# Output projection as three rounded products, squares summed on VectorE, and the second norm in four groups

## The reference, cut to what matters

```
h = RMSNorm(x) * (1 + scale1) + shift1
z = h @ w_in                      # three head groups: GLA, mLSTM, S5
x = x + gate1 * (concat[A, B, C] @ w_out)        # w_out 2048 x 2048
h = RMSNorm(x) * (1 + scale2) + shift2
x = x + gate2 * PEER(h)           # w_q 2048 x 2048, then all 16384 experts' u and v
```

## Time and profile before

| | us |
|---|---|
| median of 3 runs | 4954.34 |
| the profiled execution's own time | 4968.97 |
| its span in the profile | 4967.2 |
| output projection, first to last product | 277.6 |
| from its last product to the first block product | 67.1 |

### The profile page before, as it was taken

One profiled execution on the slowest core, in us unless ns is written; L12 is line 12 of the kernel. 1 busy time (PEld: TensorE's weight loads), 2 busy tenths in 40 slices (PEclk: granted clock), 3 DMA queues, 4 the chain that ended last, 5 costly groups with the idle time before them and its releaser, 6 DMA issues.

```text
span 4967.2 us, 68686 instructions
## 1 busy us (share of the span) xinstructions
PE 4623.2 (93%) x29440; PEld 4147.1 (83%) x29440; DVE 2422.2 (49%) x3620; ACT 1000.8 (20%) x1128; POOL 638.5 (13%) x492
## 2 busy tenths in 40 slices
PE   6799999999899699999999999999986998899898
PEld 3577777776655599999999999999976998899897
DVE  0388223114300324676777611111134888788785
ACT  1000101111100211222234411111121222222222
POOL 1000000001000000000000000000044884333330
PEclk7899999987799799999999999999987999999999
DMA  7211211146611222333334433333345999999993
GB/s 300 86 52 52 74 53 64 51 157 259 260 62 49 93 75 84 100 109 109 100 131 161 159 110 99 106 108 108 101 144 195 357 353 332 344 347 337 331 334 144
DMA packets 209254, 805.62 MB, mean 162 GB/s; under 512 B 35496, under 2 KB 101480, under 8 KB 153112
## 3 DMA queue, kind: packets, MB, share of 16 engines
q1 hardware_dynamic: 151832, 526.99, 30.3%
q0 software_dynamic: 37056, 212.73, 11.5%
q10 hardware_dynamic: 20160, 62.92, 3.1%
HBM read 724.74 MB, written 77.84 MB: 162 GB/s over the span
## 4 chain that ended last, share of the span: by engine, by line
PE 84%; DMA 8%; DVE 4%; issue 3%; ACT 1%; SPq 0%; DVEq 0%; ACTq 0%
PE PS L2061 12%; PE PS L2063 12%; PE PS L2062 12%; PE PS L1935 11%; PE PS L2041 6%; PE PS L2139 5%; PE PS L2141 5%; PE PS L2140 5%; PE PS L1938 4%; DMA arena<-in_peer_v 4%; DMA arena<-in_w_ada 3%; PE PS L1707 2%; PE PS L2113 2%; DVE arena L1630 2%; PE PS L1691 1%
## 5 line engine op out<-in xcount | busy, mean ns | idle before, releaser
L2061 PE MATMUL PS<-h_hi,blk_hi 128*128 128x288 f32 x4608 | 1368.6, 297 | 58.0 <-DVE blk_lo L1466 53.8
L2063 PE MATMUL PS<-h_hi,blk_lo 128*128 128x288 f32 x4608 | 1359.3, 295 | 0.0
L2062 PE MATMUL PS<-h_lo,blk_hi 128*128 128x288 f32 x4608 | 1359.0, 295 | 0.0
L2061 PEld LDWEIGHTS PS<-h_hi,blk_hi 128*128 128x128 f32 x4608 | 866.7, 188 | 59.0 <-issue 50.6
L2062 PEld LDWEIGHTS PS<-h_lo,blk_hi 128*128 128x128 f32 x4608 | 866.8, 188 | 0.0
L2063 PEld LDWEIGHTS PS<-h_hi,blk_lo 128*128 128x128 f32 x4608 | 866.1, 188 | 0.0
L2139 PE MATMUL PS<-co_hi,ev_hi 128*128 128x384 f32 x2048 | 702.1, 343 | 120.4 <-DVE arena L1614 100.6
L1466 DVE TENSOR_TENSOR blk_lo<-arena,blk_hi 128x2048 fp32r<-128x2048 f32 x144 | 329.9, 2292 | 820.9 <-ACT blk_hi L917 820.4
L2141 PE MATMUL PS<-co_hi,ev_lo 128*128 128x384 f32 x2048 | 698.4, 341 | 22.5 <-issue 22.5
L2140 PE MATMUL PS<-co_lo,ev_hi 128*128 128x384 f32 x2048 | 698.7, 341 | 17.6 <-issue 17.6
L1935 PE MATMUL PS<-arena 128*128 128x288 f32 x2176 | 550.0, 413 | 2.2 <-ACT arena L748 2.2
(11 more groups left out here) (427 smaller groups left out, 4126.6 us busy)
## 6 DMA issues: line engine op xcount, KB each, us to landing
arena<-in_peer_ut SPq DMA_DIRECT2D x128, 1024.0 KB, 5.4
arena<-in_peer_v SPq DMA_DIRECT2D x256, 512.0 KB
arena<-in_w_ada SPq DMA_DIRECT2D x48, 2048.0 KB, 9.3
activation_scratch<-arena ACTq DMA_DIRECT2D x128, 288.0 KB, 5.4
arena<-in_w_f SPq DMA_DIRECT2D x17, 2048.0 KB, 7.8
gate_scratch<-arena ACTq DMA_DIRECT2D x12, 2048.0 KB, 7.1
arena<-activation_scratch SPq DMA_DIRECT2D x32, 768.0 KB
arena<-gate_scratch SPq DMA_DIRECT2D x32, 768.0 KB
```

The costliest lines, as they stand in the source:

```text
L2061: mm(split(k)[:, x], hi[:, c], h_part[0][:, c, cols], start=c == 0, stop=False)
L2062: mm(split(k)[:, x], hi[:, c], h_part[1][:, c, cols], start=False, stop=False)
L2063: ins = mm(split(k)[:, x], lo[:, c], h_part[0][:, c, cols], start=False, stop=c == KC - 1)
```

## The change

What it does:

1. `mix_high`, `mix_low`: as the 16 chunks of the mixed heads become ready, ACT rounds each to `mix_hi` and DVE takes the rest as `mix_lo`. Six are done in the input projection's stage, one behind each of heads 2 to 5 (and four more behind head 4), the last two behind head 5.
2. `out_high`, `out_low`: each w_out tile is split likewise, in four pieces of 1024 columns, `out_hi` into two new tiles, `out_lo` in place in the ring slot.
3. Three rounded matmuls per chunk in place of one plain one, in halves of 256 and 320 columns in place of 512 and 64. PE waits for `out_lo_made` and `mix_lo_made`.
4. Squares are made on ACT and added up on DVE (`add_square`) as the residual chunks come; PE does one product with ones at the end.
5. x is loaded before head 11 is done, and saved chunk by chunk. The three first w_q blocks are issued at the last product, the save of the last two chunks and the keys behind them.
6. The second norm and its split go in four groups of four chunks (`normed`, `normed_high`, `normed_low`); the first block product takes each chunk when its `h_lo` is there.

```diff
+            def mix_high(c):
+                act.wait_ge(hn_out if c < 12 else s5_mix, c + 1 if c < 12 else 3)
+                act.activation(mix_part[0][:, c], mix_raw[:, c], ACT.Copy).then_inc(mix_hi_made, 1)
+            def out_high(t):
+                act.wait_ge(ring_in[(Y_OUT + t) % 2], ring_fills(Y_OUT + t))
+                if t >= 2:
+                    act.wait_ge(prod_made, 2 * (t - 2) + 2)
+                for q in range(4):
+                    cols = slice(1024 * q, 1024 * q + 1024)
+                    act.activation(out_hi[t % 2][:, cols], ring_flat[(Y_OUT + t) % 2][:, cols], ACT.Copy).then_inc(out_hi_made, 1)
             ml_square(HEADS - 1)
+            mix_high(10)
             ml_root(HEADS - 1)
-            act.wait_ge(res_made, KC)
-            square_chunks(xres, sq2, 1)
+            out_high(0)
+            mix_high(11)
+            out_high(1)
+            for t in range(8):
+                for c in (2 * t, 2 * t + 1):
+                    act.wait_ge(res_made, c + 1)
+                    if c >= 2:
+                        act.wait_ge(sq_used, KC + c - 1)
+                    act.activation(sq2[:, c % 2], xres[:, c], ACT.Square).then_inc(sq_made, 1)
+                if t < 6:
+                    out_high(t + 2)
...
             ml_mean(HEADS - 1)
+            mix_low(10)
             head_out(11, m_rs)
+            out_low(0)
+            mix_low(11)
+            out_low(1)
+            for t in range(8):
+                for c in (2 * t, 2 * t + 1):
+                    residual(c)
+                    if c:
+                        add_square(c - 1)
+                if t < 6:
+                    out_low(t + 2)
...
-            dve.wait_ge(prod_out, 16 + 4)
             inverse_root(1, 3)
-            modulated(h2T[:, :].rearrange("p (c t) -> p c t", t=T), xres, V_NG2, 48, 64).then_inc(norm_made, 1)
-            dve.wait_ge(h_hi_made, 1)
-            tt(h_lo[:, :], h2T[:, :], h_hi[:, :].bitcast(F32), ALU.subtract).then_inc(h_lo_made, 1)
+            dve.wait_ge(x_saved, 16 * KC)
+            normed(0)
             low(0, 0)
+            for g in range(1, 4):
+                normed(g)
+                normed_low(g - 1)
+            dve.sem_inc(norm_made, 1)
+            normed_low(3)
             low(1, 1)
...
-                        for lo, w in ((0, TP), (TP, TS)):
+                        for b in range(2):
+                            out, cols = bank(2 * m + b, 0, (256, T - 256)[b]), slice(256 * b, (256, T)[b])
                             for c in MIX:
...
-                                ins = mm(flat(m)[:, lo:lo + w], ring[y % 2][:, c, P * m:P * m + P], mixT[:, c, lo:lo + w],
-                                         start=c == MIX[0], stop=c == MIX[-1])
+                                mm(out, hi[:, c, wc], mix_part[0][:, c, cols], start=c == MIX[0], stop=False)
+                                mm(out, hi[:, c, wc], mix_part[1][:, c, cols], start=False, stop=False)
+                                ins = mm(out, lo[:, c, wc], mix_part[0][:, c, cols], start=False, stop=c == MIX[-1])
-            sum_squares(sq2, 1, 3)
+            pe.wait_ge(sq_used, 2 * KC)
+            for lo, w in ((0, TP), (TP, TS)):
+                ins = mm(flat(3)[:, lo:lo + w], ones[:, :], sq_sum[:, lo:lo + w], start=True, stop=True)
...
+                        if isinstance(n, int) and n == 0 and x == 0:
+                            pe.wait_ge(h_lo_made, c + 1)
...
+            sp.wait_ge(prod_made, KC)
             for n in range(3):
                 load_block(a["w_q"][n], n, n)
+            save_x(14)
+            save_x(15)
```

More of the change, by code:

```diff
@@ L871, in _ @@
                         act.activation(rstd[:, :], rstd[:, :], ACT.Sqrt).then_inc(s5_sig, 1)
+                    if job == GLU_SUM // 2 + 1:
+                        for c in range(6):
+                            mix_high(c)
                     if job == ML_LOGS:
@@ L899, in _ @@
                     ada_tile_out(u)
+                if h >= 2:
+                    mix_high(6 + h - 2)
+                if h == 4:
+                    for c in range(12, 16):
+                        mix_high(c)
                 if h == 0:
@@ L950, in _ @@
             high(0, 0, 16)
+            for g in range(4):
+                normed_high(g)
             high(1, 1, 16)
@@ L1361, in _ @@
             ts(mq, mq, MDH ** -0.5, None, ALU.mult).then_inc(ml_pre, 1)
+            for c in range(6):
+                mix_low(c)
             dve.wait_ge(ml_cols, 1)
@@ L1443, in residual @@
+            mix_low(11)
+            out_low(1)
+            dve.wait_ge(x_in, 32)
+            def residual(chunk):
+                m = chunk % 2
+                xc, gcol = xres[:, chunk], mod[:, 32 + chunk]
+                pair = PS[:, 1024 * m:1024 * m + 1024].rearrange("p (b t) -> p b t", b=2)
+                dve.wait_ge(prod_made, chunk + 1)
+                step(tt(seqs(gate_tmp), seqs(pair[:, 1, 256:T - 256]), gcol[:, 1:NCOND].unsqueeze(2).broadcast_to([P, NSEQ, SLEN]),
                         ALU.mult))
-                stt(xc[:, 0:TP], flat(m)[:, 0:TP], gcol[:, 0:1], xc[:, 0:TP], ALU.mult, ALU.add).then_inc(prod_out, 1)
+                stt(halves(xc[:, 0:TP]), pair[:, :, 0:256], gcol[:, 0:1], halves(xc[:, 0:TP]), ALU.mult, ALU.add
+                    ).then_inc(prod_out, 1)
@@ L1459, in _, with add_square @@
[L1459 to L1460 removed]
+            def add_square(c):
+                dve.wait_ge(sq_made, KC + c + 1)
+                if c == 0:
+                    dve.tensor_copy(sq_sum, sq2[:, 0]).then_inc(sq_used, 1)
+                else:
+                    dve.wait_ge(sq_used, KC + c)
+                    tt(sq_sum, sq_sum, sq2[:, c % 2], ALU.add).then_inc(sq_used, 1)
+            for t in range(8):
+                for c in (2 * t, 2 * t + 1):
+                    residual(c)
+                    if c:
+                        add_square(c - 1)
+                if t < 6:
+                    out_low(t + 2)
@@ L1463, in low, with normed_low @@
+            def normed_low(g):
+                for c in range(4 * g, 4 * g + 4):
+                    dve.wait_ge(h_hi_made, c + 1)
+                    ins = tt(h_part[1][:, c], h2c[:, c], h_part[0][:, c].bitcast(F32), ALU.subtract)
+                    ins.then_inc(h_lo_made, 1)
             def low(n, k):
```

120 lines of the change are left out of this document (77 added, 43 removed).

## The result

The kernel before took 4955.92 us (median of 4 runs, 4951.11 to 4961.4) and the changed one 4892.10 us (median of 4, 4887.07 to 4896.05): ratio 0.9875, with 95% between 0.9862 and 0.9889. That is 63.8 us less, 28 us short of the 91.3 forecast and 2 us outside the forecast's range. The profiled execution of the changed kernel took 4890.59 us, 78.4 less than that of the kernel before.

A forecast was written before the change was run, and what follows sets the result against it. PE was taken as the bound (84% of the chain of waits). Products -77.6, start +12.5, clock +2.0 and tail -28.2 sum to -91.3 us, so the median 4954.34 becomes 4863 us, range 4843 to 4890.

The forecast's parts named there:

- the last one of the sum: Behind the tail: loads, stores and waits counted from block ends, so everything shifts, with no further gain or loss.
- The products: Output projection: 768 pairs of rounded products at 0.452 ns a column take 200.0 us in place of 277.6, -77.6.
- The bound from above: Projection: weight loads hold 256-column products at 130 ns, adding 11 us, 4874 in all; rival's chance 0.12.
- the rival in which the excess is absent: Projection: products cost their columns alone at 2.4 GHz, 184.3 us, 16 less, total 4847; chance 0.06.
- The start by its cause: Projection's start: PE's first product waits for all of `out_low(0)` behind head 11, at 1361.9 for 1349.4, +12.5 us.
- The clock behind the start: Projection's first products: after 12 us of rest PE runs at clock 0.50 for a while, losing 2.0 us.
- the rival of a lasting low clock: Projection: clock stays at 0.50 throughout, 364 us, +86 in place of -78, total 5025; chance 0.04.
- The keeping up: Projection: each next w_out tile's load and split fit in 17 of PE's 25 us per tile, hidden.
- The mix splits: Ahead of the projection: splits of the mix chunks fit in ACT's and DVE's gaps, cost 0.
- The save's wait: Tail: `x_saved` stands behind three w_q blocks and stalls the norm by 2.3 us, bounds 0 and 7.
- The tail: Last product to block 0's end: 54.0 us for 82.2, -28.2, of which 17 squares and 11 norm groups.
- the rival of a lesser tail: Tail: save holds the norm to +17 and block 0 runs at 0.50, 5 + 5 us, total 4873; chance 0.16.

The follow-up runs named there:

- the kernel with the code moved back: Changed kernel plus 124 idle semaphore increments ahead of PE's first block product, restoring its loops' earlier page positions; median 4848.16 us, ratio 0.9861.
- the first pair of profiles: Profiled executions of the kernel before and the changed kernel as first measured; medians 4955.92 and 4892.10 us, ratio 0.9875.
- The last experiment: On the changed kernel with code moved back, DVE does all four norm groups before the first block's split and the `h_lo` pieces; 4881.59 us.
- The second pair: Kernel before and changed kernel both run again, without edits, for the spread between executions; ratios 1.0001 and 0.9878.

## Why the prediction was right in direction and wrong in size

**The step that failed** is the last one of the sum: "Behind the tail all loads, stores and waits are counted from block ends, so everything shifts". Loads, stores and waits do shift; the place of PE's loops in their pages is not counted from block ends but from the program's first instruction, and the change moved it by 132. Behind block 0 that is worth +16.7 us in the profiles, -18.2 when it is taken back and +17.0 when it is put into the kernel before. Without it the profile would have come to -95. Nothing in the kernel before's profile showed a stall of that size, but the three rests of 1.6 us at the jumps were there to ask about.

**The products were mis-sized**: 206.0 us where 200.0 and 2.0 of clock were forecast. The earlier trace rows was read as 768 products of 288 columns in 100 us, 130.2 ns. In that stretch 70 of the records are short score products of 128 columns, and a count of records in a stretch also takes in the two or so under way at its start. In a stretch of block products alone (3109 to 3209 us of the kernel before) the starts are 132.5 ns apart, which is 120.0 for the columns at 2.4 GHz and 12.5 more. The 384 columns of the earlier trace rows, read from starts, take 173.5 = 160.0 + 13.5; the projection's 256 and 320 take 120.0 = 106.7 + 13.3 and 146.7 = 133.3 + 13.4. The forecast took the excess for a share of the columns, though two sizes lie too near to tell a share from a constant. The bound from above, 130 ns at 256 columns, held; the rival in which the excess is absent (184.3 us) fell. So did the gap rule that was quoted with it: "TensorE: Matmul & The Clock Gate" of the Trainium skill, Back-to-back issue gap, would give 109.2 ns at 256 columns, and the trace has 120.0. The page calls that the gap of an isolated matmul, and says that in a stream of weight loads and matmuls both set the spacing; every product here has a load of its own.

**What was right.** The start by its cause: PE rests 11.8 us ahead of its first product, forecast 12.5, in every version with that order, and moving `out_low(0)` ahead of head 11 takes 5.6 us of it back. That the first product came at 1360.99 for a forecast of 1361.9 is in part luck: in the versions with the same 11.8 us it comes anywhere from 1354.7 to 1363.7. The clock behind the start: twelve products at 213 ns and a loss of 1.4 us, 2.5 us in the kernel with the code moved back, forecast 2.0; the rival of a lasting low clock fell (0.99 over the projection). The keeping up: no wait for `out_lo` in 206 us. The mix splits: without the 11.8 us of rest the stages ahead of the projection moved by 0.1 us in the first pair of profiles and by 3 in the second, where they came out shorter, so no cost of the splits shows, and a us of it could not be seen. The save's wait: 2.9 us, forecast 2.3, and 1.7 to 2.5 in three of the other profiles. The tail: block 0's end at 54.6, forecast 54.0, so 27.7 saved and not 28.2, and the rival of a lesser tail fell. Its larger part, 17 us forecast for the squares, is supported by the run with squares on PE, which gives back 12.5 (14 expected), or 15.4 with the 2.9 us wait for the save that it no longer has. The other 11 were forecast for the groups. The last experiment shows that PE's early start in block 0 has no share in them; ACT's 7.9 us rounding to `h_hi`, bare in the earlier trace rows and now beside DVE, would be most of them, but no run takes it back.

**The sum again.** -91.3, +4.1 for products and clock, -0.8 for the start, +0.5 for the tail, +16.7 for the pages: -70.8. The value stage's -7.6 makes the profiles' -78.4, so nothing of the gain was given back there. The medians have -63.8, by the ratio's interval -55 to -68. The 7 us between -70.8 and -63.8 are not placed: the profiled execution of the kernel before was 13 us over its own median, and the value stage alone differs by 33 us between the two profiles of that kernel. The second pair repeats it: the profile of the kernel before lies 15 us over its median, that of the kernel after at its own. None of the runs tells why.

## What to carry to other kernels

Where PE's program has long loops, every edit ahead of them moves their start in its page of some 250 instructions, and that alone was worth 17 us here, a quarter of what the whole change gave. The loops were of 1,750 instructions; at those of up to 870 no jump cost anything that shows. Compare the rests marked "issue" at the jumps before and after, and shift the loop with idle instructions where they are hidden, not behind a wait. To price a product, take the distance of starts within one run of equal products, not a count of records, and split it into columns and a constant before going to another size. Before building an overlap, add up the work of the engine that feeds it: where that sum is the bound, the order within it gains nothing.

## What the runs showed of the hardware that was not expected

- A jump back to the start of a loop of 1,750 instructions holds PE's sequencer for 3.3 to 3.9 us and costs PE 1.4 to 1.9 us of rest; in loops of 590 to 870 instructions the jump takes 0.2 us and no rest follows. Where the long loop starts 56 or 89 instructions (by the count above) ahead of a page's end, 2.8 to 5.2 us of rest come once more; at the first jump the second page follows the first by 6.4 to 7.0 us. With the low clock behind such rests, three jumps cost 17 us.
- A rounded product with weights of its own costs its columns at 2.4 GHz and 12.5 to 13.5 ns more: 120.0, 132.5, 146.7 and 173.5 ns at 256, 288, 320 and 384 columns.
- An instruction that only increments a semaphore takes 0.151 us of PE's sequence: 132 of them took 19.9 us, 17.8 of them bare.
